# Two modulation rows fewer in each of two mixers, four rows summed in the third mixing layer, and another order of the opening

## The reference

```
cond = silu(c)
for l in range(2):
    mod = cond @ w_ada[l] + b_ada[l]                       # 9 rows of 1024
    sh1, sc1, g1, sh2, sc2, g2, sh3, sc3, g3 = split(mod, 9)
    y = swiglu(x * (1 + sc1) + sh1, ffn1 weights)          # 1024 -> 2816 -> 1024
    x = layer_norm(ALPHA * x + 0.5 * (1 + g1) * y)
    y = token_mixer(x * (1 + sc2) + sh2, w_in, w_out)      # retention, dilated, stick-breaking
    x = layer_norm(ALPHA * x + (1 + g2) * y)
    y = swiglu(x * (1 + sc3) + sh3, ffn2 weights)
    x = layer_norm(ALPHA * x + 0.5 * (1 + g3) * y)
```

## Time and profile before

| | |
|---|---|
| median of 3 runs | 2455.41 us (2454.49 to 2457.82) |
| profiled execution | 2454.32 us, span 2452.4 us |
| TensorE busy | 2037.5 us (83% of the span) |
| VectorE busy | 1150.6 us (47%) |
| ScalarE busy | 554.5 us (23%) |
| moved by DMA | 758 MB, mean 309 GB/s over the span |
| granted TensorE clock, mean | 0.892 of full speed |

### The profile page before, as it was taken

One profiled execution on the slowest core, in us unless ns is written; L12 is line 12 of the kernel. 1 busy time (PEld: TensorE's weight loads), 2 busy tenths in 40 slices (PEclk: granted clock), 3 DMA queues, 4 the chain that ended last, 5 costly groups with the idle time before them and its releaser, 6 DMA issues.

```text
span 2452.4 us, 33654 instructions
## 1 busy us (share of the span) xinstructions
PE 2037.5 (83%) x12564; PEld 1308.0 (53%) x12564; DVE 1150.6 (47%) x1755; ACT 554.5 (23%) x885; POOL 65.5 (3%) x96
## 2 busy tenths in 40 slices
PE   5999987999799898899997877777769787666665
PEld 3998454999799645699874422222229442112111
DVE  2887676878877766877643210000026421000002
ACT  2342132433343223333332100000023110000000
POOL 1000000000000000000200000000000000000000
PEclk8999898999899899999998887777779888888887
DMA  9886774888588675688743899999996679999996
GB/s 345 301 299 251 270 260 163 283 309 313 191 291 310 225 290 198 230 311 308 266 164 140 308 409 410 410 410 410 410 385 221 239 310 410 410 410 410 410 410 268
DMA packets 290910, 758.08 MB, mean 309 GB/s; under 512 B 17616, under 2 KB 127472, under 8 KB 290720
## 3 DMA queue, kind: packets, MB, share of 16 engines
q1 hardware_dynamic: 283904, 737.34, 80.1%
q0 software_dynamic: 6688, 19.78, 2.4%
q10 hardware_dynamic: 256, 0.13, 0.0%
HBM read 756.01 MB, written 1.18 MB: 309 GB/s over the span
## 4 chain that ended last, share of the span: by engine, by line
PE 56%; DMA 21%; SPq 12%; DVE 5%; issue 3%; ACT 2%; DVEq 1%; ACTq 0%
PE psum L796 21%; DMA W<-in_w_exp_up 16%; SPq L543 10%; PE psum L808 10%; PE psum L836 5%; PE psum L857 4%; PE psum L1142 3%; PE psum L1233 3%; DMA W_mod<-in_mod_w 2%; PE psum L1035 1%; PE psum L1173 1%; PE psum L1156 1%; SPq L547 1%; PE psum L765 1%; PE psum L1188 1%
## 5 line engine op out<-in xcount | busy, mean ns | idle before, releaser
L796 PE MATMUL psum<-parts 128*128 128x256 f32 x4224 | 528.2, 286 | 17.6 <-ACT parts L1269 10.4
L796 PEld LDWEIGHTS psum<-parts 128*128 128x128 f32 x4224 | 525.7, 195 | 25.0 <-issue 18.8
L1142 PE MATMUL psum<-W,scr 128*32 128x512 f32 x1936 | 271.7, 669 | 154.6 <-DMA W<-in_w_exp_up 151.3
L1596 DVE SCALAR_TENSOR_TENSOR mod_acc<-W_mod,cond,mod_acc 128x1024 f32<-128x1024 f32 x196 | 251.8, 1285 | 50.5 <-issue 28.2
L2112 DVE TENSOR_TENSOR scr<-scr,psum 128x256 f32<-128x256 f32 x32 | 13.5, 422 | 555.1 <-ACT scr L1516 555.1
L808 PE MATMUL psum<-parts 128*128 128x512 f32 x1056 | 257.7, 393 | 0.0
L1142 PEld LDWEIGHTS psum<-W,scr 128*32 128x32 f32 x1936 | 49.4, 114 | 353.6 <-DMA W<-in_w_exp_up 275.6
L1725 DVE TENSOR_TENSOR parts<-W,parts 128x1024 fp32r<-128x1024 f32 x176 | 207.2, 1220 | 57.0 <-ACT parts L1310 57.0
L1173 PE MATMUL psum<-W,scr 128*32 128x256 f32 x2048 | 185.5, 515 | 50.3 <-DMA W<-in_w_exp_down 34.1
L808 PEld LDWEIGHTS psum<-parts 128*128 128x128 f32 x1056 | 192.6, 188 | 45.3 <-DVE parts L1738 8.2
L1310 ACT ACTIVATE parts<-W 128x1024 fp32r<-128x1024 f32 x176 | 175.9, 1051 | 78.8 <-issue 46.4
(11 more groups left out here) (299 smaller groups left out, 1686.5 us busy)
## 6 DMA issues: line engine op xcount, KB each, us to landing
W<-in_w_exp_down SPq DMA_DIRECT2D x128, 1024.0 KB
W_mod<-in_mod_w SPq DMA_DIRECT2D x123, 1024.0 KB, 5.1
W<-in_w_exp_gate SPq DMA_DIRECT2D x242, 512.0 KB, 14.9
W<-in_w_exp_up SPq DMA_DIRECT2D x242, 512.0 KB, 15.7
W<-in_ffn_w_gate SPq DMA_DIRECT2D x44, 1024.0 KB, 8.3
W<-in_ffn_w_up SPq DMA_DIRECT2D x44, 1024.0 KB, 10.8
W<-in_ffn_w_down SPq DMA_DIRECT2D x44, 1024.0 KB, 9.1
W<-in_w_in SPq DMA_DIRECT2D x24, 1024.0 KB, 8.4
```

What stands on the lines that cost most here:

```text
L796: ins = pe.matmul(psum[:, 4 + t % 2, S * g:S * g + S], w[:, t % 2, g, kc, :], u[:, kc, :], start=(n == 0 and kc == 0), stop=(n == 2 and kc ...
L1142: ins = pe.matmul(psum[32 * q:32 * q + 32, 4, :].rearrange("p (g n) -> p g n", g=2), xe_now[:, b, :], w[:, :, q, :], start=(b == 0), stop= ...
L1596: ins = dve.scalar_tensor_tensor(acc[:, :], w, col, acc[:, :], mul, add)
```

## The change

Job numbers are no longer row numbers: `MIX_ROWS`, `LOOP_ROW` and `LATE_ROWS` say which row a job sums. Each of the first two mixers sums three rows in place of five. Rows 26 to 29 (the gate of the last layer's mixer and the three rows of its experts) are summed in the third mixing layer, in 32 transfers of half a chunk (128 x 1024 numbers, 0.5 MB) that POOL issues into two halves of `k_mixer`; the next one into a half waits until VectorE has used the block there. In the opening the first gate and up weights go ahead of the last two chunks, ScalarE rounds them before it waits for the second row, and the mixers' constants are loaded behind the first gate. The core of the diff, shortened:

```diff
-JOBS_LAYER = 3 * PAIRS
+MIX_ROWS = ((7, 8, 9), (20, 30, 31))
+LOOP_ROW = (2, 10, 15, 21)
+LATE_ROWS = (26, 27, 28, 29)
+JOBS_LAYER = 2 * PAIRS + len(MIX_ROWS[0])
-MIX_BANK = (3, 3, 3, 1, 6)
-MIX_CHUNKS = {2: (0, 2), 6: (2, 8), 8: (8, 12), 10: (12, 16), 12: (16, 18)}
+MIX_BANK = (3, 3, 6)
+MIX_CHUNKS = {2: (0, 2), 6: (2, 6), 8: (6, 8), 10: (8, 10)}
...
 # SP, opening
+            def last_first_chunks():
+                first_chunk(6)
+                sp.wait_ge(mod_freed[0], 1)
+                first_chunk(7)
+                mod_bias_row(1, 1)
+            first_chunk(0)
+            sp.wait_ge(zeroed, 1)
+            mod_bias_row(0, 0, True)
+            for b in range(1, 6):
+                first_chunk(b)
+            sp.dma_start(x_tok[:, :, :], A["x"]...).then_inc(s_x, 16)
...
-                step_weights(l, k, 0, 0, max(base - 2, 1))
+                step_weights(l, k, 0, 0, max(base - 2, 1), last_first_chunks if (l, k) == (0, 0) else (lambda: None))
...
 # SP, expert 1's block for k_mixer
-            spare_slots(0, [(0, m2_done("p12")), (1, m2_done("pool1")), (2, m2_done("S15"))])
+            spare_slots(0, [(1, m2_done("pool1")), (2, m2_done("S15"))])
             first_slots(0, [(s, m2_done("out")) for s in MIXOUT_S])
+            spare_slots(0, [(0, (late_used, KC * len(LATE_ROWS)))])
...
 # POOL
+            def late_block(n):
+                row, b = LATE_ROWS[n // KC], n % KC
+                if n >= 2:
+                    pool.wait_ge(late_used, n - 1)
+                else:
+                    pool.wait_ge(m_pe.s, m_pe.at("out", LAYERS - 1))
+                pool.dma_start(late_w[n % 2], A["mod_w"][row, P * b:P * b + P, :]).then_inc(late_landed[n % 2], 16)
...
                 bias(s)
+                if s == 6:
+                    for n in range(2, KC * len(LATE_ROWS)):
+                        late_block(n)
+                    for n, row in enumerate(LATE_ROWS):
+                        pool.wait_ge(late_taken, n + 1)
+                        pool.dma_start(mod_rows[row:row + 1, :]..., late_bias[n][0:97:32, :]).then_inc(late_stored, 16)
...
 # TensorE, mixer: row_sum(2) behind project(0, 0, 0) and row_sum(3) are gone; row_sum(4) is row_sum(2)
 # TensorE, third mixing layer
+            def late_sums(first, end):
+                pe.wait_ge(late_used, KC * end)
+                ...
+                for n in range(first, end):
+                    for q in range(4):
+                        ins = pe.matmul(late_psum[n][32 * q:32 * q + 32, :], K["ones"][:, 0:32], ...)
+                ins.then_inc(pe_late, end - first)
...
+                if n == 11:
+                    late_sums(0, 2)
+            late_sums(2, 3)
...
+            pe.wait_ge(late_taken, 3)
-            times_rows(uT, lambda u: in_slot("out", MIXOUT_S[u])).then_inc(m2_pe.sig("out"), 1)
+            times_rows(uT, lambda u: in_slot("out", MIXOUT_S[u]), lambda: late_sums(3, 4)).then_inc(m2_pe.sig("out"), 1)
+            pe.wait_ge(late_taken, 4)
...
 # ScalarE, opening
+            mod_row(0, 0, first_row[0])
+            high_gate_up(0, 0, 0)
+            mod_row(1, 1, first_row[1])
...
 # VectorE, mixer
                 mixer_row(l, 0)
-                mixer_blocks(2)
+                heads(3, 7)
                 mixer_row(l, 1)
-                heads(3, 7)
-                mixer_blocks(3, 0, 2)
-                mixer_row(l, 2)
                 heads(5, 7)
                 maxima(0)
-                mixer_blocks(3, 2, 4)
                 weighted(0)
...
 # VectorE, third mixing layer
+            def late_blocks(first, end):
+                for n in range(first, end):
+                    r, b = divmod(n, KC)
+                    col = cond[:, LATE_ROWS[r], b:b + 1]
+                    dve.wait_ge(late_landed[n % 2], 16 * (n // 2 + 1))
+                    if b:
+                        dve.drain()
+                        ins = dve.scalar_tensor_tensor(late_acc[r], late_w[n % 2], col, late_acc[r], mul, add)
+                    else:
+                        ...
+                        ins = dve.tensor_scalar(late_acc[r], late_w[n % 2], col, None, mul)
+                    ins.then_inc(late_used, 1)
...
             times_gain(6)
+            late_blocks(0, KC)
...
                 dve.tensor_scalar(key_max[:, n:n + 1], ...).then_inc(m2_dve.sig(f"max{n}"), 1)
+                late_blocks(KC + n, KC + n + 1)
...
             dve.tensor_copy(uT[:, 2:4, :], part(psum[:, 5, :], 0, 2, S)).then_inc(m2_dve.sig("yT1"), 1)
+            late_row(2)
+            late_blocks(3 * KC, 4 * KC)
             plus_bias(6)
+            late_row(3)
```

More of the change, by code:

```diff
@@ L52 @@
 CTX_ROW = MOD2 + 6 * LAYERS
-JOBS = CTX_ROW + 2
+ROWS = CTX_ROW + 2
 FIRST_JOBS = 2
-JOBS_LAYER = 3 * PAIRS
-assert FIRST_JOBS + LAYERS * JOBS_LAYER == JOBS
+MIX_ROWS = ((7, 8, 9), (20, 30, 31))
+LOOP_ROW = (2, 10, 15, 21)
+LATE_ROWS = (26, 27, 28, 29)
+JOBS_LAYER = 2 * PAIRS + len(MIX_ROWS[0])
+JOBS = FIRST_JOBS + LAYERS * JOBS_LAYER
+JOB_ROWS = [0, 1]
+for l_ in range(LAYERS):
+    for k_ in range(2):
+        JOB_ROWS += [LOOP_ROW[2 * l_ + k_] + i for i in range(PAIRS)] + list(MIX_ROWS[l_] if k_ == 0 else ())
+assert sorted(JOB_ROWS + list(LATE_ROWS)) == list(range(ROWS)) and len(JOB_ROWS) == JOBS
 MIX_IN_USES = IN_W * D // (P * 2048)
@@ L262, in build @@
         pooledT = part(att_0, 0, 4, S)
+        late_w = [k_mixer[:, D * n:D * n + D] for n in range(2)]
+        late_acc = [part(qm[:, 8:12, :].rearrange("p a b -> p (a b)"), 0, D), tmp[:, 0, :], tmp[:, 1, :],
+                    part(qm[:, 8:12, :].rearrange("p a b -> p (a b)"), 0, D)]
+        late_bias = [mod_bias[:, :], mix_bias[1], mod_acc[:, 512:768], mod_acc[:, 768:1024]]
+        late_psum = [psum[:, 2, 0:256], psum[:, 2, 256:512], psum[:, 3, 0:256], psum[:, 6, 0:256]]
         ctx_tok = part(qm[:, 4:12, :].rearrange("p a b -> p (a b)"), 0, TT, D)
@@ L302, in build @@
         sel = carve(6656, TT, EXPERTS * CAP)
+        late_landed = [sem(f"late_block_landed{n}") for n in range(2)]
+        late_used = sem("late_blocks_used")
+        late_bias_in = sem("late_bias_landed")
+        pe_late = sem("late_rows_in_psum")
+        late_taken = sem("late_rows_taken")
+        late_stored = sem("late_rows_stored")
         s_const = sem("constants_loaded")
+        s_mixer_const = sem("mixer_constants_loaded")
         s_cvec = sem("conditions_loaded")
@@ L635, in columns @@
                 if need is not None:
-                    pool.wait_ge(mod_stored, need)
+                    rows_stored(range(need))
                     pool.wait_ge(zeroed, 3)
@@ L1580, in _, with mod_blocks @@
             mul, add, sub = ALU.mult, ALU.add, ALU.subtract
-            def mod_blocks(job, done, b0, b1, acc=mod_acc):
+            def mod_blocks(job, row, done, b0, b1, acc=mod_acc):
                 for b in range(b0, b1):
```

157 lines of the change are left out of this document (88 added, 69 removed).

## The result

The changed kernel takes 2463.8 us (median of 11 runs, 2457.9 to 2468.5), the kernel before 2454.75 in the same rounds (11 runs, 2452.9 to 2459.6). The ratio is 1.0036, with a 95% interval of 1.0028 to 1.0045: 8.8 us slower, 6.9 to 11.0. Forecast were 2462.4 and slower. The profiled run of the changed kernel is the slowest of its eleven (2468.54, span 2466.7), so its span stands 14.3 above that of before where the medians differ by 9.

A forecast was written before the change was run, and what follows sets the result against it. TensorE, with 56% of the chain of waits, was taken as the main bound, the third layer included. Terms -1.8 - 13.4 + 5.2 + 10 + 0.4 + 6.6 = +7.0 on the median 2455.4 gave 2462.4 us, range 2444 to 2480.

The forecast's parts named there:

- The opening: Start of the kernel: first FFN matmul at 44.1 in place of 45.93 us, a gain of 1.8.
- The mixers: First two mixers: two rows fewer remove TensorE's waits and two sums each, 5.4 and 8.0 us, together -13.4.
- what is late next: First mixer: VectorE's masks for the first stick-breaking pair, ready about 1 us before TensorE asks, so no new gap.
- The first eight blocks: Third layer, ahead of the second tile's squares: late transfers delay the rope and TensorE by 5.2 us; bounds 0 to +8.3.
- The attention: Third layer's 16 steps: block supply of 2.83 us replaces steps of 2.19; +10 for the last product, bounds +1.4 to +30.
- The third row's taking and the output product: Third layer's end: +0.4 for taking the row, +6.6 for a mid-product gap of 4.4, sums and clock.
- The clock's 1.6: Output product, third layer: TensorE loses 1.6 us to the clock with the gap between halves, by a mixer's precedent.
- k_mixer's expert block: Behind the output product: one more MB loaded during TensorE's routing work costs nothing, or 2.6 us without free DMA time.
- the blocks come in VectorE's shade: Rival, third layer: landing under 2.9 us, only 1.4 + 0.4 + 0.6 paid, 2442.6; chance 0.28 including half-way cases.
- the clock falls in the attention's steps: Rival, third layer: TensorE's lower clock in five to thirteen steps costs 8 to 20 us more, 2470 to 2482; chance 0.1.
- a mixer gives half back: Rival, first two mixers: another wait replaces the weighting's, 6.7 us lost again, 2469; chance 0.07.
- transfers stay at 7 us with empty queues: Rival, third layer: late transfers take nearer 7 than 4 us, up to 2490; chance 0.05.

The follow-up runs named there:

- kernel 1: The kernel before with only the new opening (order of first chunks, weights rounded earlier, mixer constants moved out); ratio 0.9999.
- Kernel 9: The kernel before, with the third and fourth block of the mixers' fourth row put behind the weighting of the first scores on VectorE; ratio 1.0000.
- kernel 10: The kernel before, all five rows kept; fourth row's first blocks and third row's taking put behind heads and maxima, its next blocks behind the weighting; ratio 0.9967.
- Kernel 5: The changed kernel with the first expert's 3 MB of down weights asked for behind the output product; ratio 1.0024 to the kernel before.
- kernel 6: The changed kernel with four buffers and late blocks moved: 4 ahead of the squares, 16 in the attention's steps, 12 under the output product; ratio 0.9960.
- Kernels 3 and 4: Both from the changed kernel: the first keeps all 32 sums but transfers only two blocks, ratio 0.9950; the second has four buffers from the ninth block, 0.9993.
- kernel 8: The changed kernel with 16 late blocks of the attention's steps asked for by ScalarE's hardware queue in place of POOL; ratio 1.0035 to the kernel before.
- kernel 2: The changed kernel without the late rows' blocks, sums and transfers, only their biases stored; ratio 0.9934 to the kernel before.

## Why the prediction was right, point by point

The number held, and so did the mechanism of the loss, the supply through two buffers. But of its terms one was mis-sized by a factor of two, one had the wrong cause, and two errors cancelled in part; that it came so near the measured time is in part luck.

**The opening (-1.8).** Right at the place: the first FFN matmul stands at 42.8 to 44.9, mean 43.9, in the eleven profiles with the new order that were taken, and at 45.9, 45.7 and 44.9 in three with the old one. In the timing of the opening alone it doesn't show. One reading was off: the row at 25.54, given as 1.94 at the slow clock, is 1.80; in the changed kernel the last chunks do take 1.94 and 1.93.

**The mixers (-13.4).** Right in size: the nine profiles with three rows have mixer stages of 161.6 and 162.8 us on average, against 169.2 and 169.1 in the two of before and of kernel 1 (from the mixer's first projection to the next FFN's first matmul): -7.6 and -6.3, together -13.9. Each alone was foreseen as -5.4 and -8.0; the split is off. The cause was wrong. "Which wait for VectorE's weighting behind the fourth row's blocks" took the instruction just ahead for the reason. Kernel 9 moved these blocks away and gained nothing. VectorE came late to the heads and the maxima already, behind the fourth row's first two blocks, which wait 3.79 for their chunk, and the third row's taking; kernel 10 moved those and had 8 us. That "what is late next", the masks, makes no new gap held.

The stretch between the mixers (first matmul of the second FFN to the second mixer) takes 417.0 on average in these nine and 417.7 (416.9 to 418.2) in the five others. It was not foreseen, and chance is not excluded.

**The first eight blocks (+5.2): the step that failed in size.** The term stands at TensorE's first matmul behind the rope, 35.01 behind the gain before and 44.92 after: +9.9, over its bound of 8.3 (the rope's end, foreseen 6.7 later, came 11.2 later). What failed is the transfer time in it. The bound took 7.1 as the most that a transfer takes under full engines; the first pair took 11.3 and 12.4. (The same rows had 7.8 as a maximum, which would not have been enough either.) The 7.1 are from a place where one transfer of POOL stood alone; here gain_row's 0.5 MB had been asked for 0.66 us earlier and four column transfers before it, beside SyncE's 3 MB of down weights. Kernel 5 shows those 3 MB as 6 of the 11 us; the other half is not separated. The late squares then left TensorE idle for 10.60 us, and at the lower clock it lost another 2.9 up to the first maximum, 1.7 of them on the pooled matmuls (5.33 against 3.62), which was not in the sum. In kernel 6, with only four blocks there, the first maximum comes 40.89 behind the gain, as before.

**The attention (+10).** +8.8: 46.05 from the first maximum to the last product in place of 37.22 (the earlier trace rows give its end; the first maximum stood at 1259.64). Steps of 2.71 on average from 1265.03 to 1297.60, 2.83 foreseen, since the transfers took 3.8 on average there, not 4.0 (the prediction's own round trip, 0.30 + 4.0 + 1.33, is 5.63 and not 5.66, which moves nothing). They make 6.3 of the 8.8; 0.6 more came in the first three steps and 1.9 behind the last maximum, most of it from the lower clock there, which the term did not have. Kernels 3 and 4 separate supply and sums: the same twelve steps take 2.32 on average in both.

The Trainium skill's "DMA: Bandwidth & Descriptors" gives, in "Anatomy of one DMA — SWDGE (gpsimd) path", an estimate of 3.2 for this size; the fastest transfer of the thirty took 3.4, the median 3.8. The same page puts the first byte of a hardware queue 0.4 us earlier ("Specifications"); kernel 8 doesn't bear that out for the round trip, with a median of 4.1. The page's account that most of a transfer's fixed part is the receipt of the last byte, not the asking, is not contradicted by kernel 8, where another engine's asking made nothing shorter; the receipt itself no run here shows.

**The third row's taking and the output product (+0.4, +6.6).** Together +4.7 in the product and 1.4 ahead of it. The gap is 3.35 (4.4), the sum 0.57. The clock's 1.6 did not come behind the gap, the second half took 14.00; it came ahead of it. At the end of the steps ScalarE and TensorE waited for VectorE, whose last blocks were late (TensorE 2.02 us), and the clock fell to its lower level; from 1296 to 1309 it is 0.63 on average, and the last products took 3.51 in place of 1.99. With four buffers the same wait is 0.55 and the clock 1.00 from 1282 to 1326. So the two terms' 7.0 were 6.1; a precedent from one place in a kernel did not say where the clock falls in another.

**k_mixer's expert block (0).** Right: from the end of the output product to the first product with it 45.5, before 45.6. The expert loop behind it only moved, as foreseen.

**The sum.** By the stage, 27.5 for the late work (against kernel 2) in place of the 22.2 of the four terms; -13.9, -1.6 and -0.7 ahead of it in place of -15.2. That makes +11.3, just over the measured +6.9 to +11.0, and what stands between is not settled: the times alone give 25 for the late work. The prediction's +7.0 came out near because the late work was sized 5 too low and the stretches ahead 1 too small.

**The rivals.** That the blocks come in VectorE's shade needed a landing under 2.9 us, and none of the thirty was faster than 3.4. Its price can be read from kernel 3, which has the sums without the transfers: 0.6 by the stage where 2.4 was foreseen. That its whole, 2442.5 by its ratio of times, is the 2442.6 foreseen is luck; the interval is 3 us to either side. That the clock falls in the attention's steps: in 1262 to 1296 it is 1.00 although TensorE is busy for 31.79 of 34.00 us only, with the work of 2.19 us spread over steps of 2.71. The second failure mode in the Trainium skill's "TensorE: Matmul & The Clock Gate" would let it swing there; this trace doesn't show it. In this layer it was low only in and behind the 10.60 us without work, and from the end of the steps into the output product; behind the gap of 3.35 there it did not fall. That a mixer gives half back, or that transfers stay at 7 us with empty queues: neither came.

## What to carry to other kernels

A transfer that is asked for when its buffer comes free costs its whole round trip over the number of buffers, here (0.3 + 3.8 + 1.3) / 2 = 2.7 us for each block; price it by buffers and by the place in the queue, and try two more buffers before moving the work: here they took 13 of the stage's 27 us (10.5 by the times), in space that was free. Where an engine waits ahead of an instruction, follow that engine's own timeline back to its first idle stretch before naming the instruction in front as the cause: of two edits of one order, the one that moved the work just in front gave nothing, the one that also moved the chunk wait a few instructions earlier gave 8 us, within the intervals as much as the best version that moved four whole rows. And a bound from a transfer that stood alone is none for one that is asked for right behind others.

## What the runs showed that I had not expected

A half-MB transfer into 128 partitions, with little else than the late block beside it under way, took no less in ScalarE's hardware queue (3.3/4.1/4.9 us) than in POOL's software queue (3.4/3.7/5.1). Right behind another half MB of the same queue and beside 3 MB of SyncE it took 11.3 and 12.4, without the 3 MB 8.9 and 8.8. TensorE's clock stayed at the upper level through the attention's steps, with 6.5% of idle time in short pieces (31.79 of 34.00 us busy from 1262 to 1296, granted clock 1.00), but was at the lower one at their end, behind 2.02 us of waiting.
